# The scan of each SSD group set in front of the next transposes, its skip term on ScalarE, its exponents in one block

## The reference, cut to what matters

```python
xbc = jax.nn.silu(causal_dwconv(xbc, ssm_conv_w, ssm_conv_b))
xs, bm, cm = jnp.split(xbc, ...)                     # x, B, C
dt = jax.nn.softplus(dt_raw + ssm_dt_bias); a_neg = -jnp.exp(ssm_A_log)
acs = jnp.cumsum(dt * a_neg, axis=1)                 # one chunk of 256 tokens
decay = jnp.exp(jnp.where(causal, acs[:, :, None] - acs[:, None, :], -jnp.inf))
cb = jnp.einsum('blgn,bsgn->blsg', cc, bc)
y = jnp.einsum('blsg,blsgh,bsghp->blghp', cb, decay, xs * dt) + ssm_D * xs   # scan and skip term
v = y * jax.nn.silu(z)                               # then a norm over each group
```

## Time and profile before

| | |
|---|---|
| Median of three runs | 685.7 us (685.39 to 686.08) |
| The profiled execution's own time | 685.14 us |
| Its span | 683.3 us |
| Mean granted TensorE clock | 0.997 |
| TensorE busy (matmul) | 673.6 us, 99% |
| VectorE busy | 493.9 us, 72% |
| ScalarE busy | 370.2 us, 54% |
| DMA moved | 130.92 MB, mean 192 GB/s |

### The profile page before, as it was taken

One profiled execution on the slowest core, in us unless ns is written; L12 is line 12 of the kernel. 1 busy time (PEld: TensorE's weight loads), 2 busy tenths in 40 slices (PEclk: granted clock), 3 DMA queues, 4 the chain that ended last, 5 costly groups with the idle time before them and its releaser, 6 DMA issues.

```text
span 683.3 us, 11411 instructions
## 1 busy us (share of the span) xinstructions
PE 673.6 (99%) x4505; PEld 616.5 (90%) x4505; DVE 493.9 (72%) x616; ACT 370.2 (54%) x461; POOL 9.9 (1%) x22
## 2 busy tenths in 40 slices
PE   8999999999999999999999999999999999999996
PEld 6999999999999988899888888888899999999995
DVE  6886979696866766777755655556688777777796
ACT  6668767767455544555533333443466555555552
POOL 0000000000100000000000000000000000000001
PEclk9999999999999999999999999999999999999998
DMA  9785767569195456545566665665436555555521
GB/s 297 236 266 172 247 202 257 159 223 326 62 265 175 144 164 232 173 150 168 170 218 215 217 191 182 196 229 173 169 124 207 186 185 187 188 185 186 193 82 62
DMA packets 99505, 130.92 MB, mean 192 GB/s; under 512 B 5649, under 2 KB 73742, under 8 KB 98830
## 3 DMA queue, kind: packets, MB, share of 16 engines
q1 hardware_dynamic: 97926, 125.27, 56.3%
q10 hardware_dynamic: 1544, 5.16, 2.1%
HBM read 129.31 MB, written 2.68 MB: 193 GB/s over the span
## 4 chain that ended last, share of the span: by engine, by line
PE 96%; DVE 1%; ACT 1%; DMA 1%; POOL 0%; issue 0%; POOLq 0%; SPq 0%; DVEq 0%; ACTq 0%
PE ps L364 30%; PE ps L365 30%; PE ps L366 30%; PE ps L674 1%; DMA x_nat<-x 1%; PE ps L711 1%; PE ps L659 1%; PE ps L419 1%; PE ps L675 1%; PE ps L694 1%; DVE w_lo L336 0%; DVE h_nat L1733 0%; PE ps L702 0%; PE ps L693 0%; ACT w_hi L332 0%; PE ps L713 0%
## 5 line engine op out<-in xcount | busy, mean ns | idle before, releaser
L336 DVE TENSOR_TENSOR w_lo<-w_raw,w_hi 128x2048 fp32r<-128x2048 f32 x107 | 244.6, 2287 | 90.8 <-ACT w_hi L332 90.8
L332 ACT ACTIVATE w_hi<-w_raw 128x2048 fp32r<-128x2048 f32 x107 | 204.3, 1910 | 100.7 <-PE ps L366 93.9
L364 PE MATMUL ps<-tok_hi,w_hi 128*128 128x256 f32 x864 | 247.0, 286 | 0.7 <-DVE tok_lo L1295 0.7
L365 PE MATMUL ps<-tok_lo,w_hi 128*128 128x256 f32 x864 | 244.5, 283 | 0.0
L366 PE MATMUL ps<-tok_hi,w_lo 128*128 128x256 f32 x864 | 244.5, 283 | 0.0
L364 PEld LDWEIGHTS ps<-tok_hi,w_hi 128*128 128x128 f32 x864 | 165.7, 192 | 2.3 <-issue 0.9
L365 PEld LDWEIGHTS ps<-tok_lo,w_hi 128*128 128x128 f32 x864 | 165.8, 192 | 0.4
L366 PEld LDWEIGHTS ps<-tok_hi,w_lo 128*128 128x128 f32 x864 | 165.7, 192 | 0.0
L364 PE MATMUL ps<-w_hi,tok_hi 128*128 128x512 f32 x128 | 50.2, 392 | 0.0
L365 PE MATMUL ps<-w_lo,tok_hi 128*128 128x512 f32 x128 | 49.9, 390 | 0.0
L366 PE MATMUL ps<-w_hi,tok_lo 128*128 128x512 f32 x128 | 49.8, 389 | 0.0
(11 more groups left out here) (266 smaller groups left out, 1000.7 us busy)
## 6 DMA issues: line engine op xcount, KB each, us to landing
w_raw<-w_in SPq DMA_DIRECT2D x94, 512.0 KB, 4.8
w_raw<-w_ffn_up SPq DMA_DIRECT2D x44, 512.0 KB, 4.4
w_raw<-w_ffn_down SPq DMA_DIRECT2D x22, 512.0 KB, 3.9
w_raw<-w_mem_kv SPq DMA_DIRECT2D x16, 512.0 KB, 4.5
w_raw<-w_br_ssm SPq DMA_DIRECT2D x16, 512.0 KB, 4.9
acs_b<-acs_d ACTq DMA_DIRECT2D x4, 1024.0 KB, 6.6
w_raw<-w_br_attn SPq DMA_DIRECT2D x8, 512.0 KB, 4.9
w_raw<-w_br_mem SPq DMA_DIRECT2D x8, 512.0 KB, 4.5
```

Source lines behind the costliest of these rows:

```text
L332: act.activation(w_hi[:, s, :], w_raw[:, s, :], ACT.Copy).then_inc(hi_ready[s], 1)
L336: dve.tensor_tensor(w_lo[:, s, :], w_raw[:, s, :], w_hi[:, s, :].bitcast(F32), ALU.subtract).then_inc(lo_ready[s], 1)
L364: pe.matmul(o, a[0], b[0], start=start, stop=False, **kw)
L365: pe.matmul(o, a[0], b[1], start=False, stop=False, **kw)
```

## The change

On TensorE `rest_of_group` now makes z0 and z1, then calls the decay sums (group 0) or the scan of the group before (groups 1 to 3), then the transposes. On ScalarE the skip term D·x is written to `y_sum` by four scaled copies (`skip`), and VectorE's `scan_out` becomes one addition over 1024 elements of both banks and the product with `z_act`; it stands behind `activate(1)` and `activate(2)` now. All exponents of a group are behind both z halves: for groups 1 to 3 the first token tile's behind the z splits, the second tile's behind the qm split; for group 0 both behind the qm split. The copies and DMAs of the decay sums (`acs_away`) are behind z1's split, and `load_acs(0)` behind `skip`. `sum_squares` stands before the qm remainder. The last scan, in the attention stage, keeps its place.

```diff
--- before.py
+++ after.py
@@ -9,6 +9,8 @@
 
 
 
+
+import functools
 
 import numpy as np
 
@@ -649,10 +651,11 @@
                 pe.matmul(row[SHEADS:2 * SHEADS], da_s[:, 1, :], tri_wide[:, 0:P], start=False,
                           stop=True).then_inc(acs_mm, 1)
 
-            def rest_of_group(g, between=None):
+            def rest_of_group(g, sums):
                 r = 2 * g + 1
-                gemm_cols(pe, r, 0, tok_hi, tok_lo, between=between)
+                gemm_cols(pe, r, 0, tok_hi, tok_lo)
                 gemm_cols(pe, r, 1, tok_hi, tok_lo)
+                sums()
                 pe.wait_ge(conv_done, 3 * g + 3)
                 for t in range(NT):
                     for c in range(GT):
@@ -681,8 +684,7 @@
                 gemm_cols(pe, 2 * g, 0, tok_hi, tok_lo)
                 gemm_cols(pe, 2 * g, 1, tok_hi, tok_lo)
                 gemm_cols(pe, 2 * g, 2, tok_hi, tok_lo)
-                scan(g)
-                rest_of_group(g)
+                rest_of_group(g, functools.partial(scan, g))
 
 
             def scores(i):
@@ -1003,58 +1005,64 @@
                         act.wait_ge(bias_mm, 1)
                         act.activation(bias_row[0:2 * Q + HEADS, :], ps[0:2 * Q + HEADS, 5, 0:P],
                                        ACT.Copy).then_inc(bias_copied, 1)
-                    if first and s == 2:
-                        act.wait_ge(acs_mm, 1)
-                        act.activation(acs_s[:].rearrange("p t h -> p (t h)"), ps[:, 7, 0:NT * SHEADS],
-                                       ACT.Copy).then_inc(acs_ready, 1)
-                        act.activation(acs_row[0:2 * SHEADS, :], ps[0:2 * SHEADS, 7, T:T + P],
-                                       ACT.Copy).then_inc(acs_ready, 1)
-                        act.wait_ge(acs_ready, 2)
-                        for t in range(NT):
-                            act.dma_start(acs_d[:, t * P:(t + 1) * P],
-                                          acs_row[t * SHEADS:(t + 1) * SHEADS, :]).then_inc(acs_out, 16)
                     act.wait_ge(conv_step, 18 * g + 6 * s + 6)
                     act.activation(tanh_a[:, s], conv_a[:, s], ACT.Tanh).then_inc(conv_tanh, 1)
-                if not first:
-                    exponents(g, 0, range(0, HPG // 2))
-                    if not last:
-                        load_acs(g + 1)
                 for s in range(2):
                     act.wait_ge(gemm_done[s], r + 2)
                     act.wait_ge(conv_done, 3 * g + s + 1)
                     act.activation(tanh_a[:, s], halves(s), ACT.Tanh, scale=0.5).then_inc(z_tanh, 1)
                     split_hi(act, r + 2, s)
-                    if first:
-                        if s == 0:
-                            act.wait_ge(acs_out, 16 * NT)
-                            load_acs(0)
-                        for t in range(NT) if s else ():
-                            exponents(g, t, range(HPG))
-                            if t == 0:
-                                load_acs(1)
-                    elif s == 0:
-                        exponents(g, 0, range(HPG // 2, HPG))
-                    else:
-                        squares(g)
-                        exponents(g, 1, range(HPG))
+                if first:
+                    acs_away()
+                    skip(g)
+                    act.wait_ge(acs_out, 16 * NT)
+                    load_acs(0)
+                else:
+                    exponents(g, 0)
+                    if not last:
+                        load_acs(g + 1)
+                    squares(g)
+                    skip(g)
                 act.wait_ge(gemm_done[2], r + 2)
                 act.activation(qm[:, bass.ds(2 * g, 2), :], halves(2), ACT.Copy).then_inc(bank_free[2], 1)
                 split_hi(act, r + 2, 2)
+                if first:
+                    exponents(g, 0)
+                    load_acs(1)
+                exponents(g, 1)
                 act.wait_ge(seg_ready, 2 * g + 2)
                 act.activation(decay[:], decay[:], ACT.Exp, scale=-1.0).then_inc(decay_ready, 1)
 
-            def exponents(g, t, heads):
+            def acs_away():
+
+                act.wait_ge(acs_mm, 1)
+                act.activation(acs_s[:].rearrange("p t h -> p (t h)"), ps[:, 7, 0:NT * SHEADS],
+                               ACT.Copy).then_inc(acs_ready, 1)
+                act.activation(acs_row[0:2 * SHEADS, :], ps[0:2 * SHEADS, 7, T:T + P],
+                               ACT.Copy).then_inc(acs_ready, 1)
+                act.wait_ge(acs_ready, 2)
+                for t in range(NT):
+                    act.dma_start(acs_d[:, t * P:(t + 1) * P],
+                                  acs_row[t * SHEADS:(t + 1) * SHEADS, :]).then_inc(acs_out, 16)
+
+            def skip(g):
+
+                act.wait_ge(conv_done, 3 * g + 3)
+                for c in range(GT):
+                    a = act.activation(y_sum[:, c, :], conv_o[:, 2 + c, :], ACT.Copy,
+                                       scale=cols_skip[:, bass.ds(GT * g + c, 1)])
+                a.then_inc(y_step, 1)
+
+            def exponents(g, t):
 
                 act.wait_ge(acs_in, 16 * g + 16)
-                if heads[0] == 0 and t == 0:
-                    act.wait_ge(y_mm, g)
+                act.wait_ge(y_mm, g)
                 c, first = ((slice(0, T), 0), (slice(T, T + P), P))[t]
-                for h in heads:
+                for h in range(HPG):
                     at = bass.ds(HPG * g + h, 1)
                     a = act.activation(decay[:, h, c], acs_b[:, at, first:T].squeeze(1), ACT.Relu,
                                        bias=acs_s[:, t, at], scale=-1.0)
-                if heads[-1] == HPG - 1:
-                    a.then_inc(seg_ready, 1)
+                a.then_inc(seg_ready, 1)
 
             def squares(n):
 
@@ -1355,13 +1363,11 @@
 
             def scan_out(n):
 
+                dve.wait_ge(y_step, 2 * n - 1)
                 dve.wait_ge(y_mm, n)
-                for c in range(GT):
-                    dve.scalar_tensor_tensor(y_sum[:, c, :], conv_o[:, 2 + c, :],
-                                             cols_skip[:, bass.ds(GT * n - GT + c, 1)],
-                                             ps[:, 6 + c // 2, (c % 2) * T:(c % 2 + 1) * T], ALU.mult,
-                                             ALU.add).then_inc(y_step, 1)
-                dve.wait_ge(y_step, GT * n)
+                both = y_sum[:].rearrange("p (b c) t -> p b (c t)", b=2)
+                dve.tensor_tensor(both, ps[:, 6:8, :], both, ALU.add).then_inc(y_step, 1)
+                dve.wait_ge(y_step, 2 * n)
                 dve.scalar_tensor_tensor(v_ssm[:, bass.ds(GT * n - GT, GT), :], z_act[:], 0.5, y_sum[:], ALU.mult,
                                          ALU.mult).then_inc(v_ready, 1)
 
@@ -1404,10 +1410,11 @@
                 convolve(2)
                 split_lo(dve, r + 1, 2)
                 if not first:
+                    activate(1)
+                activate(2)
+                if not first:
                     scan_out(g)
                     dve.wait_ge(v_ready, g)
-                    activate(1)
-                activate(2)
                 silu_z(0)
                 silu_z(1)
                 dve.wait_ge(xg_turned, g + 1)
@@ -1418,13 +1425,13 @@
                                       ALU.mult).then_inc(xdt_ready, 1)
                 dve.wait_ge(cb_mm, g + 1)
                 dve.tensor_tensor(cb[:], ps[:, 5, 0:3 * P], cb_mask, ALU.mult).then_inc(cb_masked, 1)
+                if not first:
+                    sum_squares(g)
                 split_lo(dve, r + 2, 2)
                 dve.wait_ge(cb_masked, g + 1)
                 dve.wait_ge(decay_ready, g + 1)
                 dve.tensor_tensor(decay[:], decay[:], cb[:].unsqueeze(1).to_broadcast([P, HPG, 3 * P]),
                                   ALU.mult).then_inc(decay_cb, 1)
-                if not first:
-                    sum_squares(g)
 
             def sum_squares(n):
 
```

## The result

The changed kernel takes 693.68 us (median of 4 runs, 693.03 to 694.65); the kernel before, on the same chip, 685.55 us. The ratio is 1.0124, with a 95% interval of 1.0112 to 1.0136: 8.1 us slower. I had forecast slower, 689.4 us with a range to 691.8. The way was right, the size was not.

What follows compares the result with a forecast made beforehand. TensorE was taken to bound the kernel. 0 from switches, 3.7 us from the wait in front of z0 of group 1 and 0 from the rest gave 688.8 profiled, 689.4 against the median, range 687.4 to 691.8.

Steps and rivals of the forecast that it cites:

- What bounds the kernel: TensorE's matmuls fill 673.6 of the 683.3 us span, so only taking work or switches off TensorE wins time.
- no gain comes from the switches: Switches behind decay sums and three scans: bounds 0.8 us won and 0; taken as 0, since the transposes pay.
- The place and the mechanism: z0 of group 1 waits once for VectorE's split of slot 0, behind group 0's late decay product: 3.7 us.
- steps 1 to 5: Group 0's delayed chain from z1's product through copies, write, read and exponents to the split, ending at 71.5.
- The asked-for time: z0 of group 1 is asked for at 67.85, where the scan stood before.
- the margins of the later groups: Later groups cost 0: 0.5 us to spare at the last scan, 1.6 at z0 of groups 2 and 3.
- Step 3: Write of group 0's decay sums lands 3.4 us after its issue, at 48.5, with the skip term inside that wait.
- Step 4: Group 0's 1 MB broadcast read, issued at 48.5, takes the median 6.6 us and lands at 55.1.
- Rival A: The clock falls in z0's wait; one return costs 1.3 us, giving 690.7; chance 0.25.
- My row: Price of a clock return, from the kernel's start: 14 matmuls took 4.5 us, later 3.2 in all, so 1.3 us.
- My other bound: Estimate for the clock's fall in z0's wait: up to half of the wait again, 1.9 us.
- my plain case: A wait of 2.2 to 4.9 us at full clock in front of group 1's z0: 689.4 us, chance 0.52.

Runs made afterwards that it cites:

- e2: Changed kernel with the decay sums' old road and group 0's exponents in front of qm again: 685.04 us, ratio 0.9998.
- e1: Changed kernel with only the decay sums' making, copies, write and group 0's broadcast read back at their old places: 686.92 us, ratio 1.0023.
- e3: Changed kernel with the scans put back in front of z0, the late decay of group 0 kept: 688.29 us, ratio 1.0044.
- e5: Changed kernel with SyncE holding back group 1's z and qm weight loads until group 0's acs_b read has landed: 686.87 us, ratio 1.0026.
- e6: Changed kernel with only TensorE's decay sums back between the halves of z0's first product, ScalarE as changed: 692.32 us, ratio 1.0102.
- e8: Kernel of e2 with the skip term back on VectorE and scan_out in its old form and place: 705.57 us, ratio 1.0293.
- e9: Changed kernel with group 1 written out and 10 plain matmuls of zeros in front of its z0: 691.10 us median.
- e7: Changed kernel with group 1 written out and 20 plain matmuls of zeros in front of its z0: 690.30 us, ratio 1.0070.

## Why the prediction was right in its way and wrong in its size

**What bounds the kernel, and that no gain comes from the switches: right.** The transposes behind a narrow scan pay 0.16, the groups kept their length, and e2 equals the kernel before. The Trainium skill, page "TensorEngine Tiling (Array Packing)", section "Key Properties", has this drain at a change of the tiling mode; the trace agrees, with 1.03 against 0.87.

**The place and the mechanism: right.** z0 of group 1 waits for VectorE's split of slot 0, behind group 0's decay product; the wait occurs once, and e1, e2 and e3 take it apart as steps 1 to 5 have it. The asked-for time (67.9), the copies (44.4), the chain of 16.5 us from the first exponent to the split, and the margins of the later groups held. The decay product of the last scan began at 184.31 and took 3.3, and the scan came at 188.1: the 0.5 to spare. How thin that is e3 shows, with 0.4 us of wait there.

**Step 3, the write: wrong.** This is the term of the sum that failed. I took 3.4 us from the one write of before. It took 5.4. That row had its own company of transfers, and I moved the write beside others: the weight load of slot 0, which z0's split releases, issued 0.9 us before it, and that of slot 1 at about 46.9. e5 shows 2.8 with neither of them; e6 shows the same landing with a later issue, which speaks for the first of the two. 2.1 us of the miss.

**Step 4, the read: off.** I took the median, 6.6, of four loads that took 5.1 to 7.8. The profile had 7.4, other executions 5.1 to 6.4, so this was inside the bounds; 0.8 us in the profile compared. The two together made a wait of 6.7 out of 3.7, above the 4.9 that I had given as the longest.

**Rival A, the clock: the case, left out of the sum, and priced too low.** I gave it 0.25 and 1.3 us for one return. The clock fell with waits of 4.6 us and more in each of the profiles (the changed kernel twice, e6, e8 with three), and in the one profile at 3.1 (e9); at 1.6 and below (the profiles of e1, e3, e5, e7) it did not. The price, with the restart, was 1.8 to 2.9 us. My row, the matmuls of zeros at the start, was the wrong one: no stretch of the trace before shows the granted clock low there, and it would not tell how much of a low stretch lay before it. My other bound, up to half of the wait again, 1.9, was nearer. The Trainium skill, page "TensorE: Matmul & The Clock Gate", section "What's actually happening", says that the clock falls after an idle stretch; the rows here agree, and I had the row of the fall 2.9 us behind the last matmul in hand. With a wait of 3.7 forecast, that row should have made A the likelier case, not the smaller.

Of the 8.1 us, my plain case had 3.7. The write adds 2.1, the read 0.8 and the clock with the restart 2.2, in the profiled execution (8.9).

## What to carry to other kernels

When a piece of work is moved on the engine that bounds the kernel, look for what it covered: the next thing in line is asked for earlier, and its whole supply chain must be that early too. Do not combine this with a delay on the same chain; each half alone cost 0 or 3.1 us here, both together 8.1. Do not take the duration of a small transfer from its old row, but look at what is in flight at its new place: the same two 16 KB writes took 2.8, 3.4, 4.2 or 5.4 us (e5, before, e6, changed). And when a forecast wait on TensorE comes near 3 us, add about 2 us for the matmuls behind it (1.8 to 2.9 in these runs).

## What was not expected of the hardware

The landing of a 16 KB write did not move with its issue (44.8 or 45.9, landed at 50.6 and 50.5), and came at 47.9 when the weight loads beside it were held back. And a wait of 3.1 us could cost nearly as much again in slow matmuls (2.9 us), more than a wait of 4.9 did (1.8).
